# Four edits in a fused two-block transformer kernel: the attention gate by tanh, conv taps behind the last slot, token-half sums by products

## What is computed

```
# first block, attention branch
probs = softmax(q k^T * scale + decay, causal);  o = probs @ v
y_att = o * silu(z);          z = h @ W_za
merged = sigmoid(g_ssm)*(y_ssm @ W_s) + sigmoid(g_att)*(y_att @ W_a)
# second block, layer 0
h = x @ pw1_w + pw1_b;  a, g = split(h);  h = a * sigmoid(g)
h = causal_dwconv(h, 31 taps) ; h = silu(layer_norm(h)) ; mix = h @ pw2_w
x = layer_norm(ALPHA*x + mix)
x = layer_norm(ALPHA*x + ffn(x) + ple(x))     # stage "down0", layer 1 ends in "down1"
```

## Time and profile before

| | us |
|---|---|
| median of 3 runs | 1985.84 (1985.04 to 1987.46) |
| profiled execution, its own time | 1985.59 |
| its span | 1983.9 |
| PE busy | 1900.5 |
| DVE, ACT, POOL busy | 1055.6, 765.6, 172.0 |

### The profile page before, as it was taken

The page is one execution under the profiler, slowest core; times in us unless marked ns, Lnnn a source line. Parts: engine busy times, 40 slices in busy tenths (PEclk is TensorE's granted clock), DMA queues, the critical chain, the costliest instruction groups (busy, mean ns, idle before and its releaser), DMA issues.

```text
span 1983.9 us, 23266 instructions
## 1 busy us (share of the span) xinstructions
PE 1900.5 (96%) x9212; PEld 1530.9 (77%) x9212; DVE 1055.6 (53%) x1274; ACT 765.6 (39%) x987; POOL 172.0 (9%) x123
## 2 busy tenths in 40 slices
PE   5999999999999997999999999899999999999996
PEld 4767788877788765888888888788777888888885
DVE  6874342245435787745555533543675545555434
ACT  5532332245324545442222222643673622222223
POOL 4500000000001454010000000200000200000001
PEclk9999999999999998999999999999999999999998
DMA  9211223211132454122322233131102123232321
GB/s 393 85 64 47 88 100 106 85 64 43 64 106 85 130 137 133 64 85 85 106 87 103 97 115 106 64 106 64 43 1 96 64 85 106 85 106 88 124 89 61
DMA packets 31052, 186.45 MB, mean 94 GB/s; under 512 B 3329, under 2 KB 5505, under 8 KB 10498
## 3 DMA queue, kind: packets, MB, share of 16 engines
q1 hardware_dynamic: 29392, 175.96, 26.4%
q10 hardware_dynamic: 1586, 9.44, 1.2%
HBM read 174.64 MB, written 2.10 MB: 89 GB/s over the span
## 4 chain that ended last, share of the span: by engine, by line
PE 89%; ACT 4%; DVE 3%; issue 2%; DMA 1%; POOL 1%; ACTq 0%; DVEq 0%
PE PS L588 25%; PE PS L589 25%; PE PS L590 24%; PE PS L1095 2%; PE PS L980 2%; PE PS L656 1%; PE PS L658 1%; PE PS L657 1%; DMA RAW<-w 1%; PE PS L949 1%; PE PS L930 1%; PE PS L1066 1%; PE PS L1069 1%; ACT WH L1141 1%; PE PS L1106 1%
## 5 line engine op out<-in xcount | busy, mean ns | idle before, releaser
L588 PE MATMUL PS<-H,WH 128*128 128x512 f32 (+1 forms) x1616 | 624.8, 387 | 27.0 <-POOL L L452 13.5
L589 PE MATMUL PS<-L,WH 128*128 128x512 f32 (+1 forms) x1616 | 617.7, 382 | 0.0
L590 PE MATMUL PS<-H,WL 128*128 128x512 f32 (+1 forms) x1616 | 617.6, 382 | 0.0
L1708 DVE TENSOR_TENSOR WL<-RAW,WH 128x2048 fp32r<-128x2048 f32 x136 | 313.2, 2304 | 268.1 <-ACT WH L1141 263.8
L588 PEld LDWEIGHTS PS<-H,WH 128*128 128x128 f32 x1616 | 305.8, 189 | 99.0 <-issue 18.5
L1141 ACT ACTIVATE WH<-RAW 128x2048 fp32r<-128x2048 f32 x144 | 274.8, 1909 | 227.2 <-PE PS L590 187.3
L590 PEld LDWEIGHTS PS<-H,WL 128*128 128x128 f32 x1616 | 305.7, 189 | 58.9
L589 PEld LDWEIGHTS PS<-L,WH 128*128 128x128 f32 x1616 | 305.8, 189 | 56.9 <-issue 0.5
L452 POOL TENSOR_TENSOR L<-X,H 128x512 fp32r<-128x512 f32 x32 | 46.6, 1464 | 1303.6 <-ACT H L1511 745.3
L1580 ACT ACTIVATE TT<-TT 128x512 f32<-128x512 f32 x44 | 27.8, 632 | 310.3 <-DVE TT L2361 310.3
L588 PE MATMUL PS<-FH,WH 128*128 128x512 f32 (+1 forms) x376 | 142.8, 380 | 0.0
(11 more groups left out here) (348 smaller groups left out, 2479.5 us busy)
## 6 DMA issues: line engine op xcount, KB each, us to landing
RAW<-w SPq DMA_DIRECT2D x148, 1024.0 KB, 4.9
HS<-HC SPq DMA_DIRECT2D x32, 264.0 KB, 5.0
ADA<-w_ada ACTq DMA_DIRECT2D x4, 1024.0 KB, 25.4
ADA<-w_ada SPq DMA_DIRECT2D x4, 1024.0 KB, 22.9
GA<-w_gate SPq DMA_DIRECT2D x1, 4096.0 KB, 18.3
PWR<-w_ple ACTq DMA_DIRECT2D x2, 1024.0 KB, 5.3
out<-X SPq DMA_DIRECT2D x8, 256.0 KB, 2.1
X<-x_t SPq DMA_DIRECT2D x2, 512.0 KB, 6.5
```

What stands on the lines that cost most here:

```text
L588: nc.tensor.matmul(ps, wh, xh, start=start, stop=False, skip_group_check=skip)
L589: nc.tensor.matmul(ps, wh, xl, start=False, stop=False, skip_group_check=skip)
L590: return nc.tensor.matmul(ps, wl, xh, start=False, stop=stop, skip_group_check=skip)
L1708: v.tensor_tensor(WL[:, p], RAW[:, p], WH[:, p].bitcast(F32), ALU.subtract).then_inc(w_lo, 1)
```

## The change

Gate: ACT writes tanh(z/2) to `ZA` instead of silu(z), at steps 8, 16, 24 and after the loop instead of at 12, 20, 28 and after it; DVE multiplies (tanh + 1) by z from PSUM (`za_silu`, a new instruction for each of 8 heads), and `gated` carries the factor 0.5. End of attention: five of the eight products of unit 1 of att_out's first slot stand between the last transposes and values; that slot's second weight slot is split in halves. Conv: the taps of chunk 5 stand behind slot 7, a third `HS` buffer, chunk 7's `HC` is made inside chunk 6's taps on DVE, the diagonals of chunk 7 come later on ACT. Sums: for the second token half after "down0" and "down1" PE multiplies `X` and `SQ` themselves (`ln_stats_direct`), and the four DVE additions go. DVE's loop over the conv's chunks and PE's over att_out's slots are written out.

```diff
-        HS = at("HS", A + 44, [P, 2, 4, HSW])
+        HS = at("HS", A + 41, [P, 3, 4, HSW])
...
+        def tap_bank(m):
+
+            return 7 if m == KC - 1 else 2 * ((GROUP0["pw1"] + KC - 1) % 2) if m == KC - 2 else 6
...
                 x = pair(X, p, cols(h))
                 pool.wait_ge(mr_ready, h + 1)
-                pool.wait_ge(st_acc, 2 * LN_AFTER["down1"] + 2)
+                pool.wait_ge(lst_ps, 2 * LN_AFTER["down1"] + 2)
...
                 sp.wait_ge(bank_free, GROUP0["pw1"] + m + 1)
-                if m >= 2:
-                    sp.wait_ge(cp_ps, m - 1)
+                if m >= 3:
+                    sp.wait_ge(cp_ps, m - 2)
...
-                    sp.dma_start(HS[:, m % 2, g, :], shifted).then_inc(hs_in[m % 2], 16)
+                    sp.dma_start(HS[:, m % 3, g, :], shifted).then_inc(hs_in[m % 3], 16)
...
+            def ln_stats_direct(stage):
+
+                i = SQ_OF[stage]
+                mean = MEANC.to_broadcast([P, P])
+                pe.wait_ge(lsq_used, 3 * i + 3)
+                nc.tensor.matmul(PS[:, 5, :], mean, ACC[:, 1].rearrange("p a t -> p (a t)"), start=True, stop=False,
+                                 skip_group_check=True)
+                pe.wait_ge(d_ready, D0[stage] + 3)
+                for m, done in ((KC - 2, st_acc), (KC - 1, bank_free)):
+                    nc.tensor.matmul(PS[:, 5, 0:HT], mean, X[:, m, HT:T], start=False, stop=True,
+                                     skip_group_check=True).then_inc(done, 1)
+                pe.wait_ge(lsq_ready, 5 * i + 5)
+                for u in range(2):
+                    mm = nc.tensor.matmul(PS[:, 5, HT:T], mean, SQ[:, u, HT:T], start=False, stop=True,
+                                          skip_group_check=True)
+                mm.then_inc(lst_ps, 1)
...
-                        if stats_midway and h == 0 and k == 2:
-                            ln_stats(after, 1)
+                        if stats_midway and h == 0 and k == (0 if after == "down0" else 2):
+                            if after == "down0":
+                                ln_stats_direct(after)
+                            else:
+                                ln_stats(after, 1)
...
+            def att_out_first(u, k, x):
+                g, b = SLOT0["att_out"], GROUP0["att_out"] % 2
+                if (u, k) == (1, 0):
+                    pe.wait_ge(w_lo, g + 1)
+                    pe.wait_ge(bank_free, GROUP0["att_out"] - 1)
+                i = u * KC + k
+                return product(PS[:, 2 * b + u, :], WH[:, g % 2, i, :], WL[:, g % 2, i, :], x[0][:, k, :], x[1][:, k, :],
+                               k == 0, k == KC - 1)
...
             n = NT * FOX_HEADS
             for i in range(n + 3):
                 if i < n:
                     logits(i)
                     slot_step(i, "za", (hl, hl))
+                else:
+                    for k in ((0, 1), (2, 3), (4,))[i - n]:
+                        mm = att_out_first(1, k, hl)
                 if i >= 3 and (i - 3) % NT == NT - 1:
                     values((i - 3) // NT)
                 if 2 <= i < n + 2:
                     turn(i - 2)
...
-            gemm("att_out", ((YH, YLA), hl), (ya_lo, lambda k: k + 1))
+            for u, k in [(0, k) for k in range(6)] + [(1, k) for k in range(5, KC)] + [(0, k) for k in range(6, KC)]:
+                if u == 0:
+                    pe.wait_ge(ya_lo, k + 1)
+                mm = att_out_first(u, k, hl if u else (YH, YLA))
+            mm.then_inc(slot_done, 1)
+            for j in range(1, COUNT["att_out"]):
+                slot(Step(j), "att_out", ((YH, YLA), hl))
...
-                pe.wait_ge(hs_in[m % 2], 16 * TAPS * (m // 2 + 1))
+                pe.wait_ge(hs_in[m % 3], 16 * TAPS * (m // 3 + 1))
                 if m == KC - 1:
                     pe.wait_ge(cm_done, 1)
+                elif m == KC - 2:
+                    pe.wait_ge(bank_free, GROUP0["pw1"] + KC)
                 elif m:
                     pe.wait_ge(cv_ready, m)
...
-                        mm = nc.tensor.matmul(PS[r, 6 + m // (KC - 1), :], DG[:, p, q, r],
-                                              HS[:, p, g, TAPS * q:TAPS * q + T], start=q == 0, stop=q == quads - 1,
+                        mm = nc.tensor.matmul(PS[r, tap_bank(m), :], DG[:, p, q, r],
+                                              HS[:, m % 3, g, TAPS * q:TAPS * q + T], start=q == 0, stop=q == quads - 1,
...
-                taps(m - 1)
-            taps(KC - 1)
+                if m < KC - 2:
+                    taps(m - 1)
+            for m in range(KC - 3, KC):
+                taps(m)
...
-            ln_stats("down1", 1)
+            ln_stats_direct("down1")
...
                 act.wait_ge(slot_done, SLOT0["za"] + j + 1)
-                act.wait_ge(bank_free, GROUP0["za"] + j)
                 b = (GROUP0["za"] + j) % 2
-                a(ZA[:, 2 * j:2 * j + 2, :], PS[:, 2 * b:2 * b + 2, :], ACT.Silu).then_inc(bank_free, 1)
+                a(ZA[:, 2 * j:2 * j + 2, :], PS[:, 2 * b:2 * b + 2, :], ACT.Tanh, scale=0.5).then_inc(za_tanh, 1)
...
                     ins.then_inc(w_hi, 1)
+                elif g == SLOT0["att_out"] + 1:
+                    ins.then_inc(w_half, 1)
...
-                if i % KC == 4 and j:
+                if i % KC == 0 and 0 < i < n:
...
+                if i == n:
+                    half_hi(SLOT0["att_out"] + 1, 0)
...
+            za(COUNT["za"] - 1)
+            half_hi(SLOT0["att_out"] + 1, 1)
             gated_hi(FOX_HEADS - GATE_LAG)
-            za(COUNT["za"] - 1)
             for m in range(FOX_HEADS - GATE_LAG + 1, FOX_HEADS):
                 gated_hi(m)
...
+            slots("att_out", att_out, head=2, split_first=False)
...
                 if m == KC - 1:
+                    whole_square(KC - 3)
+                    diagonals(KC - 1)
                     whole_square(KC - 2)
                 split_hi(Step(0), 1, SLOT0["pw1"] + m + 2)
                 if 2 <= m < KC - 1:
                     whole_square(m - 2)
-                if m + 1 < KC:
+                if m < KC - 2:
                     diagonals(m + 1)
-                if m == KC - 2:
-                    whole_square(KC - 3)
...
             n = NT * FOX_HEADS
+            def za_silu(m):
+
+                j, u = divmod(m, 2)
+                b = 2 * ((GROUP0["za"] + j) % 2) + u
+                if u == 0:
+                    dve.wait_ge(za_tanh, j + 1)
+                    dve.wait_ge(bank_free, GROUP0["za"] + j)
+                ins = v.scalar_tensor_tensor(ZA[:, m, :], ZA[:, m, :], 1.0, PS[:, b, :], ALU.add, ALU.mult)
+                if u:
+                    ins.then_inc(bank_free, 1)
...
-                v.tensor_tensor(QK[:, m, :], QK[:, m, :], ZA[:, m, :], ALU.mult).then_inc(ya_ready, 1)
+                v.scalar_tensor_tensor(QK[:, m, :], QK[:, m, :], 0.5, ZA[:, m, :], ALU.mult, ALU.mult).then_inc(ya_ready, 1)
...
-                if half == 0:
+                if half == 0 and g == SLOT0["att_out"] + 1:
+                    dve.wait_ge(w_half, 1)
+                else:
                     dve.wait_ge(w_hi, g + 1)
...
+                if i % KC in (1, 2) and KC < i < n:
+                    za_silu(2 * (i // KC - 1) + i % KC - 1)
...
+            half_lo(SLOT0["att_out"] + 1, 0)
             dve.wait_ge(ot_ready, FOX_HEADS - 1)
+            za_silu(FOX_HEADS - 2)
+            za_silu(FOX_HEADS - 1)
             gated(FOX_HEADS - GATE_LAG)
...
+            half_lo(SLOT0["att_out"] + 1, 1)
...
+            def tapped(m):
+                dve.wait_ge(cp_ps, m + 1)
+                b = tap_bank(m)
+                v.tensor_tensor(CV[:, m:m + 1, :], CV[:, m:m + 1, :], PS[:, b:b + 1, :], ALU.add).then_inc(cv_ready, 1)
+
+            def gated_in(s):
+                p = s.odd(1, GROUP0["pw1"])
+                dve.wait_ge(sig_ready, s.val(1, SIG0["pw1"] + 1))
+                free(s, "pw1", v.scalar_tensor_tensor(rows(HC, s.val(), 1)[:, :, PAD:PAD + T],
+                                                      PS[:, 2 * p:2 * p + 1, :], dcol("pw1_b", s.val()),
+                                                      TT[:, p:p + 1, :], ALU.add, ALU.mult))
...
-                dve.wait_ge(sig_ready, s.val(1, SIG0["pw1"] + 1))
-                free(s, "pw1", v.scalar_tensor_tensor(rows(HC, s.val(), 1)[:, :, PAD:PAD + T],
-                                                      PS[:, 2 * p:2 * p + 1, :], dcol("pw1_b", s.val()),
-                                                      TT[:, p:p + 1, :], ALU.add, ALU.mult))
+                if not final:
+                    gated_in(s)
...
-                    if n == (4 if final else 6) and not (isinstance(s.val(), int) and s.val() == 0):
-                        dve.wait_ge(cp_ps, s.val())
-                        before = rows(CV, s.val(1, -1), 1)
-                        v.tensor_tensor(before, before, PS[:, 6:7, :], ALU.add).then_inc(cv_ready, 1)
+                    if n == 6 and 1 <= s.val() < KC - 2:
```

(27 more changed lines are left out.)

10 lines of the change are left out of this document (5 added, 5 removed).

## The result

| | before | after |
|---|---|---|
| median | 1986.13 us | 1969.47 us |
| profiled execution, span | 1983.9 us | 1968.8 us |

The ratio is 0.9919 (0.9906 to 0.9932). Two later measurements, on two chips, gave 0.9928 (0.9914 to 0.9941) and 0.9923 (0.9909 to 0.9937); the changed kernel's 14 runs lie between 1967.6 and 1971.5, three of them above 1971.3 and so in the range.

What follows compares the result with a forecast made beforehand. PE, busy 1900.5 of 1983.9 us, was taken as the bound, so gains come only where it waits or runs at half clock. Terms 2.6 + 1.9 + 3.0 + 2.2 + 1.6 = 11.3 from 1985.59 gave 1974.3, range 1971.3 to 1979.0.

Steps and rivals of the forecast that it cites:

- Attention loop: Attention steps: silu's table loads go, removing three PE waits of 0.88 us, DVE's products hidden; 2.6 us gained.
- End of attention: Last transposes and values: att_out matmuls cover PE's waits for ACT's copies; 1.9 us gained, bounds 0.9 and 2.2.
- End of conv: Chunk 7's taps begin 2.5 us earlier, bound by ACT's diagonals, plus 0.5 from the clock; 3.0 us, bounds 2.0 and 4.3.
- The clock's 0.5: Chunk 7's taps: after a shorter PE wait, the half-clock loss falls from 1.8 to 1.3 us.
- rival (b): Matrix clock stays at 2.4 GHz after the conv's shorter wait, half-clock stretch behind the statistics shorter; 1972.0 us, chance 0.14.
- Down0 to q1: Between down0 and q1: ACT's second factor and later pairs come earlier without DVE's additions; 2.2 us, bounds 1.9 and 2.4.
- 1.6 at the end: End of kernel: without four DVE additions, scaling and ACT's outputs come earlier; 1.6 us, bounds 1.0 and 1.8.
- (a): Attention gives little: DVE late for the last slot, or the 0.88 waits return at other steps; 1978.8 us, chance 0.12.
- (c): Slower: the gate makes DVE the pacer of the attention loop; 1990.9 us, chance 0.04.
- (d): The edits don't do what they say, as when the tanh still switched tables; chance 0.04.

Runs made afterwards that it cites:

- e_tanh: Only the gate edit (tanh on ACT, product on DVE) on the kernel before; 1982.7 us.
- e_att: Both attention edits (gate and end of attention) on the kernel before, without those of the conv and the sums; median 1982.5 us.
- e_tail: Only the end-of-attention edit (five products of unit 1 moved ahead, halved split) on the kernel before, silu gate kept; median 1986.0 us.
- e_sums: Only the sums edit (second-half sums by PE's products, no DVE additions) on the kernel before; 1979.2 us.
- x_hold: Changed kernel with chunk 7's diagonals ahead of chunk 5's square, two of its four copies on ACT's queue, SP's next weight load held until they land; median 1972.0 us.
- e_conv: Only the conv edits on the kernel before; 1981.2 us.

## Why the prediction was right, and where it failed

- **Attention loop, 2.6: mis-sized.** Right in mechanism: no load, no wait, DVE's products hidden. But each stall cost 1.04, not the 0.88 of its idle row: between the two profiles the starts of the steps move by 1.04 to 1.06, 2.08 and 3.11 behind the three places, 3.1 in all, and by the same amounts in e_tanh, e_att and the second profile of after. The idle row doesn't hold all of what a stall costs; a shift of the next step's start between rows of the same kind would.
- **End of attention, 1.9: mis-sized,** 2.2, the upper bound (e_tail 2.2). The supply that I called late next with 0.6 of slack was in time: no wait.
- **End of conv, 3.0: right,** 2.8 to 3.1 to the taps between all profiles of before and after, released by the diagonals as forecast (2.5 there). The clock's 0.5 is no constant: 0.1 to 0.5 in two profiles of after (taps 6.2, against 6.3 and 6.7 before), 1.8 to 2.2 in the second (4.5). Half of rival (b) came true in that execution: the stretch behind the statistics, which (b) also wanted shorter, is 6.8 us there as before.
- **Down0 to q1, 2.2: right,** 2.2 to 2.3, and 1.6 at the end: right. e_sums alone gives both. Both half-clock stretches at q1 went in the first profile, and the stage's gain was still 2.2, since DVE's split of q1's second slot sets its end (PE's 0.4 for L1758 above). The third profile of after has a stretch at half clock there again (1251.8 to 1255.3), and the same 124.6.
- **The sum.** In the pair of first profiles the edits' own stages gave 5.3 + 2.9 + 2.2 + 1.6 = 12.0, not 11.3. The other 3.1 of 15.1 are none of my terms: 1.5 at the start, chance, and 1.5 in the stick-breaking attention, where covering two waits shows that idle time and the clock are the cause. This is the step that failed: the range added up bounds of terms, and held nothing for the clock in stages that the diff doesn't touch, though the earlier trace rows showed half clock behind waits of 2 us. That stage alone spans 99.5 to 105.1 over the kernels here. The terms' own 12.0 lie inside their bounds (8.4 to 13.3). Of the 4.8 us between forecast and median, 0.7 are the terms' own errors (0.8 too little in attention, 0.1 too much in the conv) and 1.5 this stage, nearly the 1.8 by which the range was missed; the rest is open.
- **Still open.** The medians differ by 15.3 to 16.7, 2 to 3 more than 12.0 and 1.5 together. Some of that is the taps' 1.7 in part of after's runs, and some may be the start, which moves by 3.8 from execution to execution; the rest I can't place, since only profiled executions have a trace. Nor is it settled why waits of 1.33 us take the clock down in one kernel and not in the next: after and x_hold have the same two. Shown is that with both covered it stayed up.
- Rivals (a), (c) and (d) are refuted in their stages by the rows above: DVE paces nothing, no wait came back, and no table load stands in the loop. But at the median e_att gained 2.8, not its stage's 5.3.

## What to carry to other kernels

Where PE has waits of one to some microseconds, compare the same stage across kernels and executions before you credit an edit with the difference: the stage times here agree within some 0.2 us until the clock differs. Put a term in the range for half-clock stretches in stages that the edit only shifts, both ways: two waits of 1.33 us cost from nothing to 5.5 us here, 1.5 mostly. But ask what bounds the stage before you cover a wait. Over pw2's first matmuls the stretches cost between nothing and 1.2, and at q1 0.7 at most. And a queue's order is part of a transfer's time: a copy moved to another queue lets what stood behind it start sooner, and compete with it.

## What the chip showed that I had not expected

- The clock's stretches cost up to 5.5 us in 105 at two waits of 1.33 us, and two matmuls of 0.99 us, one in each wait, took that to zero (105.08 to 99.57).
- A gain of 2.2 in its stage was worth nothing at the median (e_tail), and e_conv's 2.8 to 3.1 were worth 4.3.
- Full clock instead of half over pw2's first matmuls was worth nothing against after: 13.0 us to the 97th matmul with it, and 13.0 to 13.6 without.
- Four copies of 264 KB, started on two queues, landed within 7.0 us, and 10.9 us behind their start with a 1 MB load issued 1.6 us after them.
